# Hybrid decoder trunk: the sample tokens on two partition halves in the expert stage, one spread and one pack per expert pair, and rotary K and Q on VectorE

## What is computed

```python
def rotary(x, pos):
    half = x.shape[-1] // 2
    ...
    x1, x2 = x[..., :half], x[..., half:]
    return jnp.concatenate([x1 * cos - x2 * sin, x1 * sin + x2 * cos], axis=-1)
...
def hier_moe(h, w_rg, b_rg, w_re, b_re, w_gate, w_up, w_down):
    ...
    for e in range(N_EXPERTS):
        a = jax.nn.silu(hf @ w_gate[e]) * (hf @ w_up[e])
        y = y + gates[:, e:e + 1] * (a @ w_down[e])
    return y.reshape(shp).astype(h.dtype)
```

## Time and profile before

| | |
|---|---|
| three runs | 1720.81 us median (1719.25 to 1721.04) |
| the profiled execution | 1720.76 us, span 1718.9 us, mean granted TensorE clock 0.978 |
| TensorE matmul | busy 1618.8 us, 94% of the span |
| VectorE, ScalarE | busy 534.5 us and 298.8 us |
| from HBM | 356.48 MB, 222 GB/s over the span with the writes |

### The profile page before, as it was taken

How to read it: one execution, slowest core, us unless ns; L and a number is a source line. 1 busy time by engine, 2 the same in 40 slices (tenths; PEclk the granted TensorE clock), 3 DMA queues, 4 the chain that set the end, 5 groups by cost and what they waited for, 6 DMA issues and landing times.

```text
span 1718.9 us, 20388 instructions
## 1 busy us (share of the span) xinstructions
PE 1618.8 (94%) x8728; PEld 1010.3 (59%) x8728; DVE 534.5 (31%) x1094; ACT 298.8 (17%) x634; POOL 14.2 (1%) x30
## 2 busy tenths in 40 slices
PE   7999999889998999999999999997999899999996
PEld 4776668567765654444377675684676565445442
DVE  2024664551142311211210275645312222211122
ACT  1013322130121210001101142212202112001002
POOL 0000000000000000000000000000000000000000
PEclk9999999899999999999999999999999999999998
DMA  7223212764266399999922231237544735999993
GB/s 282 109 99 147 102 50 95 297 255 161 98 267 256 123 396 365 379 389 369 391 93 105 104 142 54 99 140 302 220 147 162 295 149 233 368 387 378 364 379 152
DMA packets 28685, 382.54 MB, mean 223 GB/s; under 512 B 3184, under 2 KB 3568, under 8 KB 3888
## 3 DMA queue, kind: packets, MB, share of 16 engines
q1 hardware_dynamic: 25040, 356.49, 53.1%
q0 software_dynamic: 3552, 24.71, 3.6%
HBM read 356.48 MB, written 24.71 MB: 222 GB/s over the span
## 4 chain that ended last, share of the span: by engine, by line
PE 84%; DMA 8%; DVE 3%; ACT 3%; DVEq 1%; issue 1%; ACTq 0%; SPq 0%; POOL 0%; POOLq 0%
PE psum L515 33%; PE psum L1084 13%; PE psum L881 8%; PE psum L1104 6%; PE psum L1069 6%; PE psum L1129 5%; DMA st_out<-states_out 4%; DMA ring<-stream 4%; PE psum L531 1%; PE psum L640 1%; PE psum L960 1%; PE psum L500 1%; PE psum L728 1%; PE psum L978 1%; PE psum L528 1%
## 5 line engine op out<-in xcount | busy, mean ns | idle before, releaser
L515 PE MATMUL psum<-h,ring 128*128 128x320 f32 x1664 | 463.3, 437 | 3.4 <-DMA ring<-stream 2.5
L515 PEld LDWEIGHTS psum<-h,ring 128*128 128x128 f32 x1664 | 316.9, 192 | 141.5 <-issue 11.8
L1084 PE MATMUL psum<-ring,work 128*64 128x512 f32 x1024 | 232.0, 597 | 1.2 <-DMA ring<-stream 1.2
L1084 PEld LDWEIGHTS psum<-ring,work 128*64 128x64 f32 x1024 | 69.6, 137 | 136.9 <-issue 130.0
L881 PE MATMUL psum<-work,ring 128*128 128x320 f32 x512 | 139.7, 433 | 0.9 <-ACT work L1251 0.9
L515 PE MATMUL psum<-mem,ring 128*128 128x256 f32 x512 | 124.4, 398 | 7.9 <-DMA ring<-stream 4.0
L1104 PE MATMUL psum<-ring,work 128*64 128x512 f32 x512 | 115.1, 602 | 7.2 <-ACT work L1491 7.2
L881 PEld LDWEIGHTS psum<-work,ring 128*128 128x128 f32 x512 | 96.5, 190 | 40.7 <-ACT work L1251 1.8
L515 PEld LDWEIGHTS psum<-mem,ring 128*128 128x128 f32 x512 | 99.8, 199 | 31.6 <-issue 12.6
L1069 PEld LDWEIGHTS psum<-work 128*128 128x128 f32 x768 | 92.7, 200 | 25.1 <-issue 25.1
L1069 PE MATMUL psum<-work 128*128 128x128 f32 x768 | 98.3, 287 | 2.2 <-DVE work L2010 2.2
(11 more groups left out here) (273 smaller groups left out, 1299.7 us busy)
## 6 DMA issues: line engine op xcount, KB each, us to landing
ring<-stream SPq DMA_DIRECT2D x168, 2048.0 KB, 9.6
st_out<-states_out POOLq DMA_DIRECT2D x18, 1024.0 KB, 10.2
mk_out<-k_mem POOLq DMA_DIRECT2D x2, 1024.0 KB, 7.8
mv_out<-work POOLq DMA_DIRECT2D x2, 1024.0 KB, 5.6
x<-x_in SPq DMA_DIRECT2D x1, 1280.0 KB, 5.9
y_out<-h POOLq DMA_DIRECT2D x2, 640.0 KB, 3.2
cst<-consts SPq DMA_DIRECT2D x1, 1270.0 KB, 22.0
mem<-mem_in SPq DMA_DIRECT2D x1, 1024.0 KB, 23.9
```

Source lines behind the costliest of these rows:

```text
L515: mm = pe.matmul(out, w[:, a:a + P], rhs[:, j, :], start=(j == 0), stop=(j == KD - 1))
L1084: mm = pe.matmul(psum[ab * CAP:(ab + 1) * CAP, up, :], h_packed[:, p % 2, k, ab * CAP:(ab + 1) * CAP], w[:, a:a + BANK], start=(k == 0), s ...
```

## The change

1. **Rotation.** The `rot` matmuls, their constant and ScalarE's eight copies are gone. VectorE reads each K or Q chunk from its projection bank with four operations in place of three: the upper 64 partitions times sin into the lower half of a scratch tile, the lower 64 times a sine of turned sign into the upper half, the whole times cos (this frees the bank), and the sum. TensorE waits for VectorE, no longer for ScalarE, before a bank of K or Q is written again.
2. **Tile 2 on two partition halves.** The 64 sample tokens keep features 0 to 511 on partitions 0 to 63 and features 512 to 1023 on partitions 64 to 127 (`rows_in`). In `pack` the third matmul of a block reads 64 partitions in place of 128. These eight matmuls stand at the end, and alternate between the halves and between banks 4 and 5. The zeroing of the unused rows goes away, and the router's small operations work on all rows in fewer instructions on VectorE and ScalarE and some more on TensorE.
3. **Order.** The spread is one group of eight behind quad 0, with four banks (2, 3, 6, 7). The pack is one group behind quad 3. On ScalarE both copies of the pack stand behind the SiLU.

```diff
-                pe.wait_ge(s_tables, 16)
-                for j in range(12):
-                    project(Q_XBC, [j])
-                    if j < 2 * RH:
-
-                        pe.wait_ge(s_evac, L * 37 + j + 1)
-                        if j >= 2:
-                            pe.wait_ge(s_rotated, L * 8 + j - 1)
-                        pe.matmul(psum[:, 4 + j % 2, 0:T], k_("rot", P), kq[:, j, :], start=True, stop=True)\
-                            .then_inc(s_rot, 1)
+                project(Q_XBC, range(12))
...
-                def pack(p, half):
+                def pack(p):
...
-                    if half == 0:
-                        pe.wait_ge(s_chosen, n_p + 1)
+                    pe.wait_ge(s_chosen, n_p + 1)
                     if p > 0:
-                        pe.wait_ge(s_packout, 2 * (n_p - 1) + half + 1)
+                        pe.wait_ge(s_packout, 2 * n_p)
+                    for half in range(2):
+                        for i in range(4):
+                            j = 4 * half + i
+                            for t in range(2):
+                                mm = pe.matmul(psum[:, 4 + half, i * P:(i + 1) * P], h_tok[:, t, j * P:(j + 1) * P],
+                                               chosen[:, p, t, :], start=(i + t == 0), stop=False, skip_group_check=True)
+                                if j + t == 0:
+                                    first(mm)
                     for i in range(4):
-                        j = 4 * half + i
-                        for t in range(3):
-                            mm = pe.matmul(psum[:, 4 + half, i * P:(i + 1) * P], h_tok[:, t, j * P:(j + 1) * P],
-                                           chosen[:, p, t, :], start=(t == 0), stop=(t == 2))
-                            if i + t == 0:
-                                first(mm)
-                    mm.then_inc(s_pack, 1)
+                        for half in range(2):
+                            j = 4 * half + i
+                            r = rows_in(2, half)
+                            mm = pe.matmul(psum[:, 4 + half, i * P:(i + 1) * P], h_tok[r, 2, j * P:(j + 1) * P],
+                                           chosen[r, p, 2, :], start=False, stop=True, skip_group_check=True)
+                            if i == 3:
+                                mm.then_inc(s_pack, 1)
...
-                        if j == 4:
+                        if j == 1:
                             pe.wait_ge(s_y1, n_p + 1)
-                        if j >= 2:
-                            pe.wait_ge(s_added, n_p * KD + j - 1)
-                        pe.matmul(psum[:, 6 + j % 2, 0:T], y_pair[:, j * P:(j + 1) * P], picked_t,
+                        if j >= 4:
+                            pe.wait_ge(s_added, n_p * KD + j - 3)
+                        pe.matmul(psum[:, SPREAD[j % 4], 0:T], y_pair[:, j * P:(j + 1) * P], picked_t,
                                   start=True, stop=True).then_inc(s_spread, 1)
...
-                        if m < 2 and p > 0:
-                            spread(p - 1, range(4 * m, 4 * m + 4))
-                        if m >= 2 and p + 1 < PAIRS:
-                            pack(p + 1, m - 2)
+                        if m == 0 and p > 0:
+                            spread(p - 1, range(KD))
+                        if m == 3 and p + 1 < PAIRS:
+                            pack(p + 1)
...
-                    if p + 1 < PAIRS:
-                        packed(p + 1, 0)
                     act.wait_ge(s_gu, n_p + 1)
                     act.activation(hidden, psum[:, 0, :], ACT.Silu).then_inc(s_sg, 1)
                     if p + 1 < PAIRS:
+                        packed(p + 1, 0)
                         packed(p + 1, 1)
...
+                half = DK // 2
+                sin = k_("sin", T)
                 for j in range(2 * RH):
-                    dve.wait_ge(s_rot, L * 8 + j + 1)
+                    dve.wait_ge(s_proj, L * 45 + KD + j + 1)
                     tmp = rot_tmp[:, j % 2, :]
-                    dve.tensor_tensor(tmp, psum[:, 4 + j % 2, 0:T], k_("sin", T), ALU.mult)
-                    dve.tensor_tensor(kq[:, j, :], kq[:, j, :], k_("cos", T), ALU.mult)
+                    own = psum[:, (KD + j) % 4, 0:T]
+                    dve.tensor_tensor(tmp[0:half], own[half:P], sin[half:P], ALU.mult)
+                    dve.tensor_tensor(tmp[half:P], own[0:half], sin[0:half], ALU.mult)
+                    dve.tensor_tensor(kq[:, j, :], own, k_("cos", T), ALU.mult).then_inc(s_vout, 1)
                     dve.drain()
                     dve.tensor_tensor(kq[:, j, :], kq[:, j, :], tmp, ALU.add).then_inc(s_rotated, 1)
```

More of the change, by code:

```diff
@@ L123, in constants @@
     put("cos", np.tile(np.cos(ang), (2, 1)))
-    put("sin", np.tile(np.sin(ang), (2, 1)))
+    put("sin", np.concatenate([np.sin(ang), -np.sin(ang)], 0))
     s, l = np.arange(P)[:, None], np.arange(P)[None, :]
@@ L419, in sum_bank, with rows_in @@
             return 0 if k == 1 or L == DEPTH else 7
+        SPREAD = [2, 3, 6, 7]
         def tok(t):
             return slice(TOK0[t], TOK0[t] + TOKN[t])
+        def rows_in(t, half):
+            return slice(0, P) if t < 2 else slice(NS * half, NS * (half + 1))
+        TILES = [(0, slice(0, P)), (1, slice(0, P)), (2, slice(0, NS)), (2, slice(NS, P))]
         def cols(t):
@@ L1021, in turn_h @@
                         pe.wait_ge(s_htout, L * 6 + 1)
-                    transposes([(psum[0:TOKN[t], i % 5, c * P:(c + 1) * P], x_routed[:, 4 * half + c, tok(t)])
-                                for c in range(4)]).then_inc(s_ht, 1)
+                    for c in range(4):
+                        out, src = psum[rows_in(t, half), i % 5, c * P:(c + 1) * P], x_routed[:, 4 * half + c, tok(t)]
+                        if i < 5:
+                            mm = pe.transpose(out, src, ident)
+                        else:
+                            mm = pe.matmul(out, src, ident, start=True, stop=True, skip_group_check=True)
+                    mm.then_inc(s_ht, 1)
                 for j in range(KD):
@@ L1039, in moe @@
                 pe.wait_ge(s_rstd, L * NNORM + 3)
-                for t in range(3):
-                    mm = pe.matmul(psum[0:TOKN[t], 5, t:t + 1], rstd[:, tok(t)], ident[:, 0:1],
-                                   start=True, stop=True)
+                for t, r in TILES:
+                    mm = pe.matmul(psum[r, 5, t:t + 1], rstd[:, tok(t)], ident[:, 0:1],
+                                   start=True, stop=True, skip_group_check=True)
                 mm.then_inc(s_rtok, 1)
                 pe.wait_ge(s_quarter, L + 1)
-                for t in range(3):
-                    mm = pe.matmul(psum[0:TOKN[t], 7, t * 32:t * 32 + EG + E], by_quarter[:, tok(t)],
-                                   k_("fold", EG + E), start=True, stop=True)
+                for t, r in TILES:
+                    mm = pe.matmul(psum[r, 7, t * 32:t * 32 + EG + E], by_quarter[:, tok(t)],
+                                   k_("fold", EG + E), start=True, stop=True, skip_group_check=True)
                 mm.then_inc(s_logit, 1)
@@ L1052, in moe @@
                 pe.wait_ge(s_rv, 2 * L + 1)
-                pe.matmul(psum[:, 7, 128:128 + 3 * E], k_("causal", P), sel[:], start=True, stop=False, skip_group_check=True)
+                pe.matmul(psum[:, 7, 128:128 + 2 * E], k_("causal", P), sel[:, 0:2, :], start=True, stop=False,
+                          skip_group_check=True)
+                for t, r in TILES[2:]:
+                    pe.matmul(psum[r, 7, 128 + 2 * E:128 + 3 * E], cst[r, CAT["causal"] + r.start:CAT["causal"] + r.stop],
+                              sel[r, 2, :], start=False, stop=False, skip_group_check=True)
                 pe.matmul(psum[:, 7, 128 + E:128 + 3 * E], ones, sel[:, 0, :].unsqueeze(1).broadcast_to([P, 2, E]),
@@ L1240, in mixer @@
                 inverse_rms(L, 0)
-                n_evac = KD
+                n_evac = 2 * KD
                 n_mem = 0
@@ L1266, in turned @@
                     nt += 1
-                for c in range(8):
-                    evac(kq[:, c, :])
                 for c in range(CC):
```

53 lines of the change are left out of this document (19 added, 34 removed).

## The result

| | before | after |
|---|---|---|
| median of the runs that came with the result | 1720.92 us (1719.25 to 1722.78) | 1696.84 us (1694.52 to 1700.63) |
| ratio, 95% interval | | 0.987 (0.9847 to 0.9894) |
| the same kernel timed again | 1720.8 us | 1697.47 us, ratio 0.9863 (0.9848 to 0.9878) |
| span of the profiled execution | 1718.9 us | 1695.0 us |

A direction and most of the mechanisms held; the amount did not.

A forecast was written before the change was run, and what follows sets the result against it. TensorE, busy for 94% of the span, was taken to bound the kernel. The terms -8.6 - 8.7 - 2.2 - 9.8 - 7.7 + 8.4 + 13.4 sum to -15.2 us, from 1720.8 to 1705.6 us, range 1699 to 1722.

The forecast's parts named there:

- Rotation, -8.6: Projection: sixteen TensorE matmuls of 0.54 us go, VectorE's work stays covered, later stages only start earlier: -8.6 us.
- Spread in one group, -8.7 and -2.2: Expert stage: four banks end TensorE's wait for VectorE's adds, -8.7 us; each layer's last spread also shortens, -2.2 us together.
- The ring, +13.4: Expert stage: TensorE waits for quad 3's load, 0.8 us in each of 14 pairs, longer in pair 0: +13.4 us.
- Shape changes, -9.8: Expert stage: 28 fewer round trips between 64-column and whole tiles on TensorE, 0.35 us each: -9.8 us.
- Row halves, -7.7: Pack: eight matmuls on 64 partitions overlap by halves, gaining 0.48 us in each of 16 packs: -7.7 us.
- Rivals 1 and 2: Pack: row halves run one after another, 1718.9 us, chance 0.23; or are slower than whole passes, 1747 us, chance 0.07.
- ScalarE's order, +8.4: Expert stage: two pack copies ahead of `hidden`'s delay down by 6.9 us, pair 0's gates by 1.5: +8.4 us.
- Rival 3: Expert stage: quad 3's refill takes as long as the longest load, waits 2.1 us every pair: 1724 us, chance 0.10.
- The router: Router: some 0.2 us gained on VectorE and as much lost on TensorE: nothing.

The follow-up runs named there:

- `order_only`: Kernel before with four spread banks, spread and pack in one group each, both pack copies behind the SiLU; whole-array tile 2, old rotation: 1712.28 us, 0.996.
- `halves_in_turn`: Changed kernel with the pack's row-half matmuls in turn, partitions 0 to 63 first, then 64 to 127, not alternating: 1699.15 us, ratio 0.9865.

## Why the prediction was right or wrong

- **What bounds it: right.** TensorE's chain gave the gain where instructions or waits left it, and the ring became the next wait.
- **Where the missing 8.9 us are.** Three places, none of them a rival of the forecast. With the clock taken out, the rotation's part gave about 11 us for 8.6 and the expert stage's about 9 for 6.6; the granted clock itself gave 2.6 to 3.7, for which the sum has no term.
- **Rotation, -8.6: a step that failed.** The projection lost the 8.6 of the sum. The sentence that what follows only "moves forward by the same 4.3 us per layer" was wrong: the part measured 10.6, 13.0, 12.3 and 14.4 us by the medians, about 11 with the clock taken out, and the stages behind layer 1's scan gain 2 us more than the clock explains. The cause stays open.
- **Spread in one group, -8.7 and -2.2: right.** 12.2 us for 10.9, and 0.62 per middle pair as summed. What lies behind a last spread was put at nothing: TensorE waited 1.40 us for VectorE there in layer 0 and 0.88 us for ScalarE in layer 1, and waits 1.15 and none after. That is 1.1 of the difference.
- **The ring, +13.4: the other step that failed, in its size.** It measured 10.2 us (11.4 against 1.2 before). The place (quad 3) is right, and so is the cause: the load was to be issued 11.3 us before it is wanted, and the trace has 11.5. The 0.8 us in each of 14 pairs were too much, as a pair waits from none to 1.6 us; and in pair 0 of layer 0 I took a load time of 9.5 us from one trace where it was 7.9, so that TensorE waited 1.16 us in place of 2.75.
- **Shape changes, -9.8: about right for one, less in sum.** `order_only` holds them with the ring: its ring wait was 11.6 us higher and its time 3.7 to 5.7, so 6 to 8 us were saved. One round trip cost 0.36 us where I took 0.35. That shape changes and ring together make +3.6 in the sum, near the measured +3.7, is luck in part: both were put too high.
- **Row halves, -7.7: overlap right.** They do run at once. In the timeline, 1.30 us lie between the start of the last whole pass and that of the first transpose; less one slot of 0.1115 that is 1.19 for the 1.78 of 16 whole passes, a gain of 0.59 per pack, or 9.5 in all. Rivals 1 and 2 fall. What I missed is what this sets off in ScalarE.
- **ScalarE's order, +8.4: right event, wrong cause, 2.4 too high.** 4.6 at down and 1.4 at the first gates came. I put it down to the moved copy; `order_only` shows that the move is free and `halves_in_turn` that the alternation of the halves makes the wait. The row halves were forecast as a gain beside this term, but their alternation makes it, and in turn or alternating, the two times can't be told apart.
- **Rival 3 (refill as late as the longest): not seen.** The load took 12.3 us in pair 2 and the waits were 0.7 us a pair, not 2.1.
- **The router: nothing**, as said. From the start of its last matmul to the first gate-and-up matmul the traces give 17.4 us before and 17.5 after, with the pack of pair 0 and the wait for its copy in it.
- **The range** took in the unknown costs of the expert stage and nothing for the granted clock or for stages that the change doesn't touch. Those differ by several us from one execution to the next, and here also in one direction.

The estimate from the Trainium skill's page "TensorE: Matmul & The Clock Gate", section "Part 3: Packing small matmuls — row/col tiling" (three quarters of the ideal overlap, 1709.0), was further off than the ideal: until the transposes start, 16 passes take 1.09 us, with the change of shape, against 1.64 in turn.

## What to carry to other kernels

When matmuls of two array halves alternate into two PSUM banks, both results are complete at the same time; if one engine copies them in turn, finish one bank first or give the copies to two engines. In a ring of few slots, look at how long before its use each load is issued: grouping quads for fewer shape changes cost 4 to 6 us here, and moving eight matmuls ahead of one quad gave about as much back. The cheapest edit, two more PSUM banks for a result that another engine adds up, gave half of the whole gain and as much as the whole new expert stage. And before two parts of a change are said to help each other, compare the granted clock of their executions.

## What the runs showed of the hardware

- VectorE takes 0.48 to 0.49 us for 320 columns on 64 partitions, also from one half of the partitions to the other, as on 128.
- Two tiles of 64 rows and 128 columns run at once even with a weight load for each pass of 128 columns: 16 float32 passes in 1.16 us, against 1.71 when neighbours use the same rows. In the changed kernel's trace the passes of the two halves start in pairs, 7 ns apart, and a pair every 0.112 us.
- A load of 2 MB lands 7.7 us after its issue when no other of the ring is under way (median of 51 in the changed kernel's trace), and 4.9 us after the one ahead when two are (median of 51).
- A stage that no edit touches can differ by 1.7 us from trace to trace because a stretch of 3.4 us at the granted clock of 0.5 (1.2 in place of 2.4 GHz) falls into it. One fell into the last down quads of layer 0 in the changed kernel's trace (8.78 us for 32 passes in place of 7.09), one into those of layer 1 in the trace before (8.77).
